# Chunks between input slots, and output projections in three rounded passes

## The reference

```python
cond = jax.nn.silu(c)
for i in range(DEPTH):
    sh1, sc1, g1, sh2, sc2, g2 = jnp.split(cond @ ada_w[i] + ada_b[i], 6, axis=-1)
    h = modulate(rmsnorm(x, norm_mix_g[i]), sh1, sc1)
    mix = gla_mixer(h, ...) if i == 0 else lru_mixer(h, ...)
    x = x + g1[:, None] * mix
    h = modulate(rmsnorm(x, norm_ffn_g[i]), sh2, sc2)
    x = x + g2[:, None] * grouped_moe(h, ...)
...
# end of gla_mixer (linear attention)
o = rmsnorm(o, norm_g) * jax.nn.silu(g).reshape(B, S, GLA_HEADS, GLA_DV)
return o.reshape(B, S, GLA_VD) @ w_out
...
# end of lru_mixer (recurrence)
y = hs.astype(h.dtype) * jax.nn.gelu(gate_br)
return y @ w_out
```

## Time and profile before

| what | value |
|---|---|
| device time, median of 3 runs | 1840.32 us (1838.58 to 1842.57) |
| the profiled execution's own time | 1840.86 us |
| its span in the trace | 1839.1 us |
| TensorE busy | 1757.2 us (96%) |
| VectorE busy | 1120.2 us (61%) |
| ScalarE busy | 738.3 us (40%) |
| moved by DMA | 392.98 MB, 214 GB/s on average |

### The profile page before, as it was taken

How to read it: one execution, slowest core, us unless ns; L and a number is a source line. 1 busy time by engine, 2 the same in 40 slices (tenths; PEclk the granted TensorE clock), 3 DMA queues, 4 the chain that set the end, 5 groups by cost and what they waited for, 6 DMA issues and landing times.

```text
span 1839.1 us, 23862 instructions
## 1 busy us (share of the span) xinstructions
PE 1757.2 (96%) x9637; PEld 1395.3 (76%) x9637; DVE 1120.2 (61%) x1626; ACT 738.3 (40%) x967; POOL 0.2 (0%) x4
## 2 busy tenths in 40 slices
PE   5899999999998989999999998999999999999999
PEld 3796777777777857777767776996754877889998
DVE  3663554446886353744447886726865664549887
ACT  3432433335665233333344666333323433034443
POOL 0000000000000000000000000000000000000000
PEclk9999899999999999999999999999999999999999
DMA  9957577767886777677786891334551332445550
GB/s 332 292 184 265 202 275 279 282 276 259 328 311 222 229 256 247 229 276 283 281 322 238 338 349 41 91 116 159 186 181 46 100 107 92 138 167 182 184 178 24
DMA packets 179029, 392.98 MB, mean 214 GB/s; under 512 B 11365, under 2 KB 102232, under 8 KB 162536
## 3 DMA queue, kind: packets, MB, share of 16 engines
q1 hardware_dynamic: 177246, 390.10, 59.7%
q10 hardware_dynamic: 1674, 1.36, 0.2%
HBM read 390.39 MB, written 1.05 MB: 213 GB/s over the span
## 4 chain that ended last, share of the span: by engine, by line
PE 85%; DVE 6%; DMA 4%; ACT 3%; issue 1%; ACTq 0%; SPq 0%; DVEq 0%
PE bank L920 19%; PE bank L948 9%; PE bank L567 9%; PE bank L1359 7%; PE bank L1157 5%; PE bank L745 5%; PE bank L1370 3%; PE bank L932 3%; PE bank L594 3%; PE bank L611 2%; PE bank L703 2%; PE bank L627 2%; PE bank L963 2%; DMA ring<-in_gla_w_in_dram 2%; DMA ring<-in_ada_w_dram 1%; PE bank L1315 1%
## 5 line engine op out<-in xcount | busy, mean ns | idle before, releaser
L2237 DVE TENSOR_TENSOR parts<-ring,parts 128x2048 fp32r<-128x2048 f32 x144 | 329.1, 2291 | 168.3 <-ACT parts L1639 167.3
L920 PE MATMUL bank<-parts 128*128 128x512 f32 x1536 | 369.7, 400 | 9.6 <-DVE parts L2313 4.0
L1639 ACT ACTIVATE parts<-ring 128x2048 fp32r<-128x2048 f32 x144 | 275.2, 1917 | 227.9 <-PE bank L920 161.6
L920 PEld LDWEIGHTS bank<-parts 128*128 128x128 f32 x1536 | 292.9, 193 | 79.2 <-issue 18.3
L1454 ACT ACTIVATE work<-bank 128x256 f32<-128x256 f32 (+3 forms) x223 | 97.5, 446 | 418.6 <-PE bank L703 68.7
L948 PE MATMUL bank<-parts 128*128 128x512 f32 x768 | 179.4, 391 | 3.7 <-DVE parts L2262 3.7
L948 PEld LDWEIGHTS bank<-parts 128*128 128x128 f32 x768 | 143.4, 188 | 36.7 <-DVE parts L2262 4.1
L567 PE MATMUL bank<-hh,ring 128*128 128x256 f32 x640 | 141.2, 380 | 2.7 <-ACT hh L1501 2.4
L567 PEld LDWEIGHTS bank<-hh,ring 128*128 128x128 f32 x640 | 121.0, 190 | 21.6 <-issue 5.5
L1359 PE MATMUL bank<-parts 128*128 128x256 f32 x1056 | 128.6, 283 | 1.4 <-DVE parts L2784 1.4
L1359 PEld LDWEIGHTS bank<-parts 128*128 128x128 f32 x1056 | 127.6, 192 | 2.2 <-issue 2.2
(11 more groups left out here) (308 smaller groups left out, 2367.5 us busy)
## 6 DMA issues: line engine op xcount, KB each, us to landing
ring<-in_moe_w_gate_dram SPq DMA_DIRECT2D x64, 1024.0 KB, 6.3
ring<-in_moe_w_up_dram SPq DMA_DIRECT2D x64, 1024.0 KB, 7.6
ring<-in_moe_w_down_dram SPq DMA_DIRECT2D x64, 1024.0 KB, 6.4
ring<-in_ada_w_dram SPq DMA_DIRECT2D x48, 1024.0 KB, 7.4
ring<-in_w_in_dram SPq DMA_DIRECT2D x32, 1024.0 KB, 5.9
ring<-in_w_mod_dram SPq DMA_DIRECT2D x24, 1024.0 KB, 7.5
ring<-in_w_up_dram SPq DMA_DIRECT2D x22, 1024.0 KB, 5.1
ring<-in_gla_w_in_dram SPq DMA_DIRECT2D x12, 1024.0 KB, 8.4
```

The source lines that it names most:

```text
L920: ins = pe.matmul(bank[:, :], xg[:, a_, k, tile * P:(tile + 1) * P], w[b_][:, j, :], start=k == 0 and n == 0, stop=k == KT - 1 and n == 2)
L1639: act.activation(moe_w[:, n % 3, 0, :], ring[:, g % RING, :], ACT.Identity)\
L2237: dve.tensor_tensor(moe_w[:, n % 3, 1, :], ring[:, (MOE_AT[layer] + AT[key]) % RING, :], moe_w[:, n % 3, 0, :].bitcast(F32), sub).then_inc ...
```

## The change

Order. One of the four chunks ahead of `gla_out`, and the norm sums, now stand ahead of the last `gla_in` slot. Three of the six chunks ahead of `lru_out` stand between the last three `lru_in` slots, one after each. The gate work of both mixers is cut into two halves of four tiles (`gla_tanh`, `cubic`, `gelu_tanh`, `gated`).

Passes. The last three slots of `gla_out` and of `lru_out` run in three rounded passes (`residual_split`); the first slot of each stays plain. `out_highs` on ScalarE and `out_lows` on VectorE split the mixer's output and the slots. All four `w_out` slots run in three passes, through the feed-forward part's buffers and its `high`, `low` and `split`; the merged tiles are split one by one.

The diff, cut to its core:

```diff
-BEFORE_LRU_OUT = [(1, i) for i in range(6, 12)]
+WITH_LRU_GATE = [(1, i) for i in range(6, 9)]
+BEFORE_LRU_OUT = [(1, i) for i in range(9, 12)]
...
-        for chunk in BEFORE_GLA_OUT:
+            if j == 10:
+                yield from mod(*BEFORE_GLA_OUT[0])
+        for chunk in BEFORE_GLA_OUT[1:]:
             yield from mod(*chunk)
...
+            yield from mod(*WITH_LRU_GATE[j - 5])
...
+            def residual_split(which, j):
+
+                n = IN_NTH[slot[0]]
+                slot[0] += 1
+                for m in range(2):
+                    pe.wait_ge(sem("in_half_low"), 2 * n + m + 1)
+                    w = in_halves_of(n, m)
+                    ps = to_dve.fill(pe)
+                    for k in range(KT):
+                        if j == 1 and m == 0 and k % 4 == 0:
+                            pe.wait_ge(sem("y_low"), 2 * which + k // 4 + 1)
+                        for i, (a_, b_) in enumerate(PASSES):
+                            ins = pe.matmul(ps[:, 0:T], w[a_][:, k, :], out_part(b_, which)[:, k, :],
+                                            start=k == 0 and i == 0, stop=k == KT - 1 and i == 2)
+                    close(to_dve, ins)
+                    in_high_used[n, m] = (to_dve.ready, to_dve.n)
                     marks["residual", which, 2 * j + m] = to_dve.n
                 free_slot(to_dve.ready, to_dve.n)
...
-            in_linear(to_act, gla_parts)
+            mod_chunk(*BEFORE_GLA_OUT[0])
             for hd in range(GLA_H):
                 norm_sum([sq[:, j, 0:T] for j in (2 * hd, 2 * hd + 1)], T)
-            for i, chunk in enumerate(BEFORE_GLA_OUT):
+            in_linear(to_act, gla_parts)
+            for i, chunk in enumerate(BEFORE_GLA_OUT[1:]):
                 mod_chunk(*chunk)
-                if i:
-                    mod_turn(7 + i)
+                mod_turn(8 + i)
             mod_turn(11)
-            pe.wait_ge(sem("gla_y"), 1)
-            for j in range(4):
-                residual_out("gla_out", lambda k: g_o[:, k, :], 0, j)
+            pe.wait_ge(sem("gla_y"), 2)
+            residual_out("gla_out", lambda k: g_o[:, k, :], 0, 0)
+            for j in range(1, 4):
+                residual_split(0, j)
...
-            for j in range(5, 8):
+            for j, chunk in enumerate(WITH_LRU_GATE):
                 linear("lru_in", to_act, h, T)
-            marks["lru_g"] = to_act.n
+                marks["lru_g", j] = to_act.n
+                if j:
+                    mod_turn(17 + j)
+                mod_chunk(*chunk)
             for i, chunk in enumerate(BEFORE_LRU_OUT):
                 mod_chunk(*chunk)
-                if i:
-                    mod_turn(17 + i)
+                mod_turn(20 + i)
             mod_turn(23)
-            pe.wait_ge(sem("lru_y"), 1)
-            for j in range(4):
-                residual_out("lru_out", lambda k: l_h[:, k, :], 1, j)
+            pe.wait_ge(sem("lru_y"), 2)
+            residual_out("lru_out", lambda k: l_h[:, k, :], 1, 0)
+            for j in range(1, 4):
+                residual_split(1, j)
...
+            ff_used.clear()
...
             for j in range(4):
-                residual_out("w_out", lambda k: g_acc[:, k, :], 2, j)
+                w = split("w_out", KT)
+                for m in range(2):
+                    ps = to_dve.fill(pe)
+                    for k in range(KT):
+                        if j == 0 and m == 0:
+                            pe.wait_ge(sem("merged_low"), k + 1)
+                        for i, (a_, b_) in enumerate(PASSES):
+                            ins = pe.matmul(ps[:, 0:T], w[a_][:, k, m * P:(m + 1) * P], merged_part(b_, k),
+                                            start=k == 0 and i == 0, stop=k == KT - 1 and i == 2)
+                    close(to_dve, ins)
+                    marks["residual", 2, 2 * j + m] = to_dve.n
+                ff_used.append((to_dve.ready, to_dve.n))
...
+            def out_highs(which, src, ready):
+
+                for half in range(2):
+                    act.wait_ge(ready, half + 1)
+                    at = slice(4 * half, 4 * half + 4)
+                    act.activation(out_part(0, which)[:, at, :], src[:, at, :], ACT.Identity).then_inc(sem("y_high"), 1)
+                n = 12 + 3 * which
+                in_high_halves(n)
+                in_high_halves(n + 1)
+                for k in range(KT):
+                    act.wait_ge(*residual_in(which)(k))
+                    act.activation(sq[:, k, 0:T], x[:, k, :], ACT.Square).then_inc(sem("sq_ready"), 1)
+                    if k == 3:
+                        in_high_halves(n + 2)
...
-            for j in range(2, 8):
-                take(g_g[:, j, :], done=j == 7 or None)
+            for j in range(2, 6):
+                take(g_g[:, j, :], done=j == 5 or None)
                 if j == 3:
                     in_high_halves(11)
-            a(act.activation(sq[:, :, T:TC], g_g, ACT.Tanh, scale=0.5), sem("gla_tanh"))
+            take_mod()
             inverses(GLA_H, GLA_DV)
-            for j in range(4):
+            a(act.activation(sq[:, 0:4, T:TC], g_g[:, 0:4, :], ACT.Tanh, scale=0.5), sem("gla_tanh"))
+            for j in range(6, 8):
+                take(g_g[:, j, :], done=j == 7 or None)
+            a(act.activation(sq[:, 4:8, T:TC], g_g[:, 4:8, :], ACT.Tanh, scale=0.5), sem("gla_tanh"))
+            for j in range(3):
                 take_mod()
-            squares(lambda k: sq[:, k, 0:T], residual_in(0))
+            out_highs(0, g_o, sem("gla_y"))
...
-            for j in range(2, 4):
-                take(l_g[:, j, :])
             act.wait_ge(sem("lru_log"), 1)
             a(act.activation(l_a, l_r, ACT.Exp))
             a(act.activation(l_m, l_r, ACT.Tanh, scale=-1.0), sem("lru_am"))
-            for j in range(4, 6):
+            for j in range(2, 4):
                 take(l_g[:, j, :])
+            take_mod()
             act.wait_ge(sem("lru_m2"), 1)
             a(act.activation(l_m, l_m, ACT.Sqrt), sem("lru_mult"))
-            for j in range(6, 8):
+
+            def gelu_tanh(half):
+
+                act.wait_ge(sem("lru_cubic"), half + 1)
+                at = slice(4 * half, 4 * half + 4)
+                a(act.activation(l_r[:, at, :], l_r[:, at, :], ACT.Tanh, scale=0.7978845608028654), sem("lru_gelu"))
+
+            gelu_tanh(0)
+            for j in range(4, 8):
                 take(l_g[:, j, :])
-            for j in range(2):
+                if j == 5:
+                    take_mod()
+            take_mod()
+            gelu_tanh(1)
+            for j in range(3):
                 take_mod()
-            act.wait_ge(sem("lru_cubic"), 1)
-            a(act.activation(l_r, l_r, ACT.Tanh, scale=0.7978845608028654), sem("lru_gelu"))
-            for j in range(4):
-                take_mod()
-            squares(lambda k: sq[:, k, 0:T], residual_in(1))
+            out_highs(1, l_h, sem("lru_y"))
...
-            squares(lambda k: f_sq[:, k, 0:T], residual_in(2))
+            for k in range(KT):
+                act.wait_ge(sem("merged"), k + 1)
+                act.activation(merged_high[:, k, :], g_acc[:, k, :], ACT.Identity).then_inc(sem("merged_high"), 1)
+            act.wait_ge(sem("merged_low"), KT)
+            high(2)
+            for k in range(KT):
+                act.wait_ge(*residual_in(2)(k))
+                act.activation(f_sq[:, k, 0:T], x[:, k, :], ACT.Square).then_inc(sem("sq_ready"), 1)
+                if k in (1, 3, 5):
+                    high(3 + k // 2)
             inverse(D)
...
+            def out_lows(which, src):
+
+                for half in range(2):
+                    dve.wait_ge(sem("y_high"), 2 * which + half + 1)
+                    at = slice(4 * half, 4 * half + 4)
+                    dve.tensor_tensor(out_part(1, which)[:, at, :], src[:, at, :], out_part(0, which)[:, at, :].bitcast(F32), sub)\
+                        .then_inc(sem("y_low"), 1)
+                for n in range(2):
+                    in_low_halves(12 + 3 * which + n)
...
-            dve.wait_ge(sem("gla_tanh"), 1)
-            stt(g_g, sq[:, :, T:TC], 1.0, g_g, add, mul)
             for hd in range(GLA_H):
                 i = inverse()
                 for j in range(2):
                     o = g_o[:, 2 * hd + j, :]
                     stt(o, o, col("gla_norm_g", j), i[:, 0:T], mul, mul)
-                    stt(o, o, 0.5, g_g[:, 2 * hd + j, :], mul, mul,
-                        done=sem("gla_y") if (hd, j) == (3, 1) else s["dve_step"])
-            for chunk in BEFORE_GLA_OUT:
+            for half in range(2):
+                at = slice(4 * half, 4 * half + 4)
+                dve.wait_ge(sem("gla_tanh"), half + 1)
+                stt(g_g[:, at, :], sq[:, at, T:TC], 1.0, g_g[:, at, :], add, mul)
+                stt(g_o[:, at, :], g_o[:, at, :], 0.5, g_g[:, at, :], mul, mul, done=sem("gla_y"))
+                if half == 0:
+                    take_mod(*BEFORE_GLA_OUT[0])
```

(36 more changed lines are left out.)

79 lines of the change are left out of this document (53 added, 26 removed).

## The result

| | before | after |
|---|---|---|
| median of the runs | 1840.38 us (1838.58 to 1842.57) | 1821.15 us (1819.74 to 1825.2, four runs) |
| profiled execution, span | 1840.86, 1839.1 us | 1820.2, 1818.3 us |
| ratio of times, 95% interval | | 0.990 [0.9885, 0.9915] |

The change makes the kernel 19.2 us faster by the medians, 20.8 by the two spans. The interval of the ratio is a gain of 15.6 to 21.2 us. Forecast were 23.7, to 1817 (own spread 1813 to 1822, range 1811 to 1829). The median lies in both, 4 us above the middle; the size of 23.7 itself lies outside the interval of this comparison.

A forecast was written before the change was run, and what follows sets the result against it. TensorE, busy 1757.2 of 1839.1 us, was taken as the bound. First output 9.0, second 11.4, mixer's output 4.3, clock -1.0 sum to 23.7: span 1815.4, forecast 1817 us (own spread 1813 to 1822, range 1811 to 1829).

The forecast's parts named there:

- Passes: Ten output slots in three rounded passes: 1.21 us saved a slot, 12.1 us in all, 3.6 for three slots.
- First output: Ahead of `gla_out`: the new order starts the first output projection at 160.7, 5.4 us earlier.
- Second output: Ahead of `lru_out`: loads under the matmuls start the second output projection at 683.2 against 690.99, 7.8 us earlier.
- ScalarE's wait: Ahead of `lru_out`: the gelu's second-half tanh delays ScalarE's chunk evictions, so TensorE waits 2.1 us at 676.7.
- The clock: Both chunk runs ahead of the outputs: each between a gain of 2 and a loss of 4; 1 us lost taken.
- The mixer's start: At `w_out`: TensorE starts on the first tiles, then waits 1.9 us instead of 1.37 for the last part.
- The experts' stages: After each mixer: work only moves earlier; a span differing from before would show the prediction wrong.
- my other signs: Signs of being right: first plain output slot starts near 161, the next layer's near 674.
- Explanation A: Posed after the result: passes and order add up; the shortfall arises ahead of `lru_out`, from later loads or late ScalarE.
- B: Posed after the result: passes or order gives nearly all, or the missing part is eaten in the experts' stages.
- stalls in the split slots: Rival, chance 0.10: rounding later than its cover, two us at each of three places, one more of slow chunks; 1824.
- Slower by half the clock in the split slots: Rival, chance 0.05: the clock granted at half in the ten split slots, 11.5 us a slot instead of 5.76; 1874.

The follow-up runs named there:

- Experiment 2: The changed kernel with chunks, norm sums and gates back in the order of before, all ten split slots kept; 1829.58 us, ratio 0.9929 to the kernel before.
- Experiment 7: The changed kernel with one more chunk moved forward in each of the first two layers; 1814.79 us, ratio 0.9842 to the kernel before.
- Experiment 4: The changed kernel with ScalarE's copies of gate tiles 2 and 3 back ahead of the decay's Exp and Tanh; 1823.42 us, ratio 0.989 to the kernel before.
- experiments 6: The changed kernel with the last three half chunks ahead of the second output loading a quarter of their bytes; 1817.39 us, ratio 0.9853 to the kernel before.
- experiment 3: The kernel before with only the mixer's output `w_out` in three rounded passes; 1838.56 us, ratio 0.9976 to the kernel before.
- experiment 8: The changed kernel with the first slot of both mixers' outputs split as well; 1827.24 us, ratio 0.9918 to the kernel before.
- experiment 10: The changed kernel with one more chunk moved forward in each of the first two layers, run again; 1816.69 us, ratio 0.985 to the kernel before.
- Experiment 5: The changed kernel with one more second-layer chunk moved forward, ahead of the gate slots; 1815.77 us, ratio 0.9858 to the kernel before.

## Why the prediction was right, and where its sizes were off

**Passes: right.** The two outputs gave 3.8 each where I had 3.6, `w_out` 4.9 where I had 4.3. The plain slot takes 6.7 to 6.8 of the 23.9 us of an output, so three split ones take 17.15, or 5.72 a slot. Experiment 2 shows it free of the order. The Trainium skill, "FP8 and Floating Point Precision" (TensorE Precision Notes), with its four passes for FP32, would have given an estimate of 17.4 for ten slots; the three outputs gave 12.5. The measurement decides: on this shape three passes aren't three quarters of the plain product.

**First output: right in kind, short in size.** Forecast 5.4, measured 4.6 over the stage, and 3.4 to 4.2 against executions of the old order without the slow clock. My sum started from before's single execution, with its 1.7 us of slow clock; where that was missing, a wait for a load of 0.52 or 0.59 came in its place, and 1.1 was gained. So about a microsecond of the 4.6 is before's one execution and not the change: luck, in this term. TensorE was ready at 161.2 (of which 1.0 came from ahead of the change), close to my 160.7. The failed part is my queue, which had the first output slot's weights in time: 159.9, 3.0 ahead of my 162.9 for the second. They landed at 162.4, that is 1.5 later if the 1.0 from ahead is taken off. Experiment 7 shows it by taking the wait away. Why this load came 4.2 us after the one ahead of it (158.2), and not 3.0, stays open.

**Second output: the term that was mis-sized.** Forecast 7.8, measured 5.6. I took the first of the last four chunk halves to land 5.1 us after its issue, "lands 5.1 us later", from the minimum in the earlier trace rows. It was issued at 664.14 and landed 6.7 us later, at 670.8, when TensorE took it. SyncE's row, that load alone in the DMA view, and all loads issued from 655 to 668 in the kernel after:

```profile
664.14 3.24 SPq L1465 DMA_DIRECT2D ring<-in_ada_w_dram  x3
...
ring<-in_ada_w_dram SPq DMA_DIRECT2D x1, 1024.0 KB, 6.7
...
DMA to landing us min/median/max: 6.7/7.9/10.3
```

In the kernel before, the four loads issued from 644 to 666 us took 5.1 to 5.3, each issued after the one ahead had landed. Here the load ahead landed only at 667.7, because the change fills the queue (295 to 373 GB/s from 650 to 660). Every later load then stood behind it, at the 2.7 that I had: the first output slot at 679.3 where my 683.2 shifts to 677.6, as the three input slots begin 5.64 earlier (638.69 against 644.33). That is 1.7 of the missing 2.2; the other 0.5 is at most what the slow clock on the transposes cost.

**ScalarE's wait: a step that failed.** "What takes the wait's place is ScalarE", 2.1 us, didn't come. I derived the new order of VectorE's work from the rows of before and left out that the change also moves Exp and Tanh of the decay ahead of two copies. The root's input was ready at 647.8, where I had 654.6 (660.28 less 5.64). Experiment 4 undoes that alone and gets a wait of 2.97. It cost some 0.3 there, since the loads were the later bound. With that order the two bounds do nearly meet, as I had it: TensorE's last row ends at 677.7 and the output's load lands at 678.1. In the kernel as it is only the loads count.

**The clock.** 1.0 us was taken off for both runs. Ahead of `gla_out` nothing shows a fall: the chunks take 1.92. Ahead of `lru_out` it fell to 0.66 and cost at most 0.5, because the output slot's load landed only at 679.3. The Trainium skill, "TensorE: Matmul & The Clock Gate" (HAM oscillation — how this bites in real kernels), says that waits for data between short bursts throttle the engine; this case's traces agree in part. The kernel after has waits of 1.18, 1.14 and 1.56 between the half chunks and a clock of 0.66. Its second execution has waits of 1.24 and 1.58 there and no fall:

```profile
673.76 1.06 PE L728 MATMUL bank<-ring,cond 128*32 128x512 f32 x8 [1.58 <-DMA ring<-in_ada_w_dram]
...
675.00:680.00 5.00, 4.25 (x23) 3.44 (x22) 3.04 (x6) 2.69 (x4) 0.00 (x0) 1.00 1.10 349
```

Experiment 4, with its wait of 2.97, has none either. So whether the clock falls there isn't told by the waits alone. The price depends on what stands there: next to nothing under a load, 1.7 us on an output slot (8.83 against 7.1 in experiments 6 and 7).

**The mixer's start: right in kind.** The wait that I forecast at 1.9 is 0.96. VectorE's last merge came 1.6 us later than before relative to TensorE, where I had 2.0, and the rounding and the low parts behind it took 0.5 where I had 1.05.

**The experts' stages.** I forecast no change, and named a different span as a sign of being wrong. After has +1.7 in the first one; but experiment 3, whose code is that of before up to `w_out`, has 398.81 there against 398.87: it is scatter, with before's single execution at the low end. As a sign this span was of no use.

**The sum.** Forecast terms 9.0, 11.4, 4.3 and -1.0; measured 8.4, 9.4, 4.9. That is 22.7 against 23.7, with 1.1 of it from before's own slow clock; and +1.0 at the start, +1.7 and -0.8 in the experts' stages make the 20.8 of the spans. Of my other signs, the first output's start was to be near 161 (162.48) and the second's near 674 (679.79); the second missed by some 5.6: 1.0 at the start, 0.8 and 2.2 in the two stages ahead of the outputs and 1.7 in the first experts' stage, less 0.2 that the first output gave more. Explanation A holds, with loads that land later than I took as its cause and not ScalarE; B doesn't. The rival "stalls in the split slots" is refuted for the change (no bracketed wait in them) and shown to be real one slot earlier (experiment 8), together with the low clock behind the stall. "Slower by half the clock in the split slots" is refuted by the 5.72 us a slot.

## What to carry to other kernels

Where a queue bounds a stretch, move loads to where the queue is idle, and then count the landing time from a queue that is already filled, not from its best case. When a change replaces one operation by several on other engines, let the first piece run in the old way: it is the cover for the start-up of the chain. Of two bounds that meet, the hidden one is worth a test by itself; it may be moved by an edit that one took for decoration. And one profiled execution is one draw: compare a stage with a second execution of the same code before the difference is called an effect.

## What was new of the hardware

- A fall of the clock can land on costly or on cheap work. In experiments 6 and 7 it lies on the first output slot (8.83 us instead of 7.07 to 7.14), in the kernel after on the last half chunk, where at most 0.6 of it shows. It isn't tied to the kernel: in experiment 10, the kernel of experiment 7, it came elsewhere, with a clock of 0.68 from 580 to 585 us at the start of `lru_in` (43.03 instead of 41.54 us), and the output took 23.95. From the start of `lru_in` to the end of the output both executions take 116.3 us (41.54 + 49.08 + 25.63 and 43.03 + 49.29 + 23.95). Experiment 5, with the same code there, had no fall at all and took 113.55:

```profile
585.00:674.00 89.00, 88.81 (x480) 67.20 (x480) 50.84 (x100) 33.30 (x57) 0.00 (x0) 1.00 0.74 250
```

- In a full queue a load of 1 MB for an output slot follows its predecessor after 3.0 us (165.42 and 168.43), one of a chunk mostly after 2.6 to 2.8. The output slots' rows are half as long (256 columns against 512); that this is the reason isn't tested.
